# Final scaling of a decoder trunk: two of the eight blocks moved from VectorE to ScalarE and GpSimd

## The chip, the cores and the metric

The kernel runs on one core of a Trainium2 chip. The metric is the device time of one execution in microseconds (us): the median of 3 runs. The profile is one execution, recorded instruction by instruction.

## The reference

Two decoder layers run over 512 positions with a model width of 1024. Each layer is a half feed-forward block, a mixer and another half feed-forward block, all added to the residual stream `x`; at the very end stands one more RMS norm with its own weights. The change is in that last step:

```python
def rmsnorm(x, w, eps=NORM_EPS):
    xf = x.astype(F32)
    y = xf * lax.rsqrt(jnp.mean(xf * xf, axis=-1, keepdims=True) + eps)
    return (y * w.astype(F32)).astype(x.dtype)

def reference(x, ...):
    for l in range(DEPTH):
        ...
        x = x + 0.5 * swiglu(rmsnorm(x, ffn_norm[l, 1]), ...)
    return rmsnorm(x, final_norm)
```

## The kernel before

The residual stream lies transposed in SBUF as `X`, 128 partitions x 8 blocks (`KB`) x 512 positions, float32: a block is 128 of the 1024 features, and a position is a column. The feature weights of the norm are then one value per partition (`PRM[:, w:w+1]`), and the reciprocal root of a position is the same for all partitions.

Each engine has one program written out by hand; they meet only at semaphores. Weights are loaded by SyncE (line 544), copied to a high part by ScalarE (`split_hi`, L1340) and to a low part by VectorE (`split_lo`, L1989), and multiplied by TensorE in three products (L614 to L616). The last feed-forward block delivers the eight blocks of `X` one after another. For each, VectorE adds the product to `X` (L2001), ScalarE squares it into `US` (L1350) and GpSimd adds the square to `ACC` (L1855); the square of the last block is not added there but summed straight from `US`.

After the last block comes a tail in which each step waits for the one before: TensorE sums the squares over the partitions (L1318 for `ACC`, L1322 for the last block), VectorE adds the two (L2669), ScalarE takes the root (L1842), VectorE the reciprocal (L2671), and TensorE spreads the 512 results over all partitions into a PSUM bank called `ROWS`, which is `GATE[0]` (L1326, semaphore `rows_ready`). Then VectorE makes each output block `HF[:, m, :]` in one instruction (L2675), and SyncE stores the blocks in order, each when it is ready (L593), and waits for the last one to land.

`GS` is a buffer in SBUF that the feed-forward blocks use for the gate and which is free at this point. `HF` takes the place of `H`, which is free too.

ScalarE loads the table of the root ahead of time, before the last block (L1499).

Of the kernel before, what the change touches and what calls it, by code (L numbers as in the profile page):

```python
# [6 lines left out]
ALU = mybir.AluOpType  # L7
ACT = mybir.ActivationFunctionType
# [7 lines left out]
KB = D_MODEL // P  # L16
# [131 lines left out]
def hybrid_trunk_kernel(nc, x, params, const, w_gate, w_up, w_down, ab_in, ab_out, lru_a, lru_x,  # L148
# [18 lines left out]
    n_norms = len(plan) + 1  # L167
    norm_cols = []
# [8 lines left out]
    with ExitStack() as ctx:  # L177
# [4 lines left out]
        def at(name, offset, shape, dtype=F32):  # L182

            words = int(np.prod(shape[1:]))
            assert offset + words <= arena_words, name
            return nc.alloc_sbuf_tensor_at(name, list(shape), dtype, offset=arena_at + 4 * offset)
# [14 lines left out]
        X = at("X", X_AT, [P, KB, SEQ])  # L201
        H = at("H", H_AT, [P, 2, KB, SEQ], F32R)
        H_PARTS = (H[:, 0], H[:, 1])
        HF = at("HF", H_AT, [P, KB, SEQ])
# [3 lines left out]
        GS = at("GS", TMP_AT, [P, 2, SEQ])  # L208
# [4 lines left out]
        PRM = at("PRM", PARAM_AT, [P, NPARAM])  # L213
# [18 lines left out]
        def sem(name):  # L232
            return ctx.enter_context(nc.semaphore(name))
# [23 lines left out]
        out_ready, stored = sem("out_ready"), sem("stored")  # L257
# [4 lines left out]
        def fits(value):  # L262

            return not isinstance(value, int) or value > 0
# [49 lines left out]
        SDEC = at("SDEC", SPARE_AT + SEQ + 96, [P, 4, CHUNK])  # L314
        KEEP = at("KEEP", SPARE_AT + SEQ + 96 + 4 * CHUNK, [P, 14])
        LAST_ROOT, LAST_RSTD, LAST_SUM, ROWS = SMALL[:, 0, :], SMALL[:, 1, :], SMALL[:, 3, :], GATE[0]
        first_sums, first_copied, sums_added, rows_ready = (sem(k) for k in ("first_sums", "first_copied", "sums_added", "rows_ready"))
        LRU_SCALE = SMALL[:, 15, :]
        LRU_NSCALE = SMALL[:, 14, :]
# [15 lines left out]
        def ab_mix(t):  # L335

            return (12, 13, *range(4, 8), *range(4), *range(8, 12))[t - 4]
# [201 lines left out]
        @block.sync  # L539
        def _(sp):  # L540
            def load(u, slot, src, cols):
                if fits(u - RING + 1):
                    sp.wait_ge(lo_ready, u - RING + 1)
                sp.dma_start(RAW[:, slot, 0:cols], src).then_inc(w_landed[slot], 16)

            sp.dma_start(PRM[:, :], params).then_inc(x_landed[0], 16)
            load(0, 0, *units[0])
            for i in range(KB // 2):
                sp.dma_start(X[:, 2 * i:2 * i + 2, :], x[:, 2 * i:2 * i + 2, :]).then_inc(x_landed[i], 16)
                if i == 0:  # L550
                    load(1, 1, *units[1])
            load(2, 2, *units[2])
            sp.dma_start(CST[:, :], const).then_inc(landed, 16)
            for phase in plan:
                u0 = base[phase]
                if phase.startswith("ffn"):
                    n = int(phase[3])
                    for j in range(0 if u0 else 3, 4):
                        load(u0 + j, (u0 + j) % RING, *units[u0 + j])
                    with sp.Fori(1, FB // 2) as i:  # L560
                        for j in range(4):
                            src = (w_gate, w_up)[j % 2][n, 2 * i + j // 2]
                            load(u0 + 4 * i + j, (u0 + j) % RING, src, KB * P)
                    u1 = u0 + 2 * FB
                    with sp.Fori(0, KB // 2) as i:
                        for j in range(4):
                            src = w_down[n, 2 * i + j // 2, :, (j % 2) * UNIT:(j % 2 + 1) * UNIT]
                            load(u1 + 4 * i + j, (u1 + j) % RING, src, UNIT)
                else:
                    count = AB_BLOCKS if phase == "ab" else C_BLOCKS  # L570
                    for j in range(count + KB):
                        if phase == "ab" and j == RING:

                            sp.wait_ge(unit_done, u0)
                            for half in range(2):
                                rows = slice(half * CHUNK, (half + 1) * CHUNK)
                                sp.wait_ge(lw_zero, 1)
                                for k, w in enumerate((lru_a, lru_x)):
                                    sp.dma_start(LW[rows, k, :, rows], w[half]).then_inc(small_weights, 16)
                            sp.dma_start(WA2[:, :], rwkv_wa).then_inc(small_weights, 16)  # L580
                            sp.dma_start(G2[:, :], rwkv_g).then_inc(small_weights, 16)
                        if phase == "c" and j == RING:
                            sp.wait_ge(unit_done, u0)
                            sp.dma_start(CT[:, :, :], c_tail).then_inc(c_tail_landed.sem, 16)

                        if phase == "ab" and j == count:
                            for s in range(2):

                                sp.wait_ge(xx_mm[s], 10)
                        load(u0 + j, (u0 + j) % RING, *units[u0 + j])  # L590
            for m in range(KB):
                sp.wait_ge(out_ready, m + 1)
                sp.dma_start(out[m], HF[:, m, :]).then_inc(stored, 16)  # L593
            sp.wait_ge(stored, 16 * KB)

# [735 lines left out]
        def _(act):  # L1331
# [10 lines left out]
            def square(n, i, j):  # L1342

                if j == 0 and fits(KB // 2 * n + i):
                    act.wait_ge(acc_ready[0], KB // 2 * n + i)
                if j == 1 and fits(odd_sums(n) + i):
                    act.wait_ge(acc_ready[1], odd_sums(n) + i)
                    if n:
                        act.wait_ge(sum_ready, n)
                act.activation(US[:, j, :], X[:, 2 * i + j, :], ACT.Square).then_inc(sq_ready[j], 1)  # L1350

            def residual(n, i, j):

                act.wait_ge(x_ready[j], KB // 2 * n + i + 1)
                square(n, i, j)
                if n < n_norms - 1:
                    act.wait_ge(hw_ready[j], KB // 2 * n + i + 1)
                    act.activation(H[:, 0, 2 * i + j, :], GS[:, j, :], ACT.Copy).then_inc(hhi_ready[j], 1)
# [68 lines left out]
            for i in range(KB // 2):  # L1427
                act.wait_ge(x_landed[i], 32 if i == 0 else 16)
                for j in range(2):
                    w = norm_cols[0] + 2 * i + j  # L1430
                    act.activation(H[:, 0, 2 * i + j, :], X[:, 2 * i + j, :], ACT.Copy,
                                   scale=PRM[:, w:w + 1]).then_inc(hhi_ready[j], 1)
# [12 lines left out]
            for phase in plan:  # L1445
# [55 lines left out]
                if phase == "ab":  # L1501
# [24 lines left out]
                    for t in range(1, AB_BLOCKS):  # L1526
# [7 lines left out]
                        if 4 <= t < 18:  # L1534
                            act.wait_ge(z_read, t + 1)
                            if t == 14:
                                act.wait_ge(norm_sum_mm, 4)
                            act.activation(ab_place(t), PAD[:, t % 2, 3:3 + SEQ], ACT.Copy,
                                           scale=KEEP[:, ab_mix(t):ab_mix(t) + 1]).then_inc(z_kept, 1)
# [289 lines left out]
                if phase in ("ab", "c"):  # L1829

                    c0 = base[phase] + (AB_BLOCKS if phase == "ab" else C_BLOCKS)
                    act.wait_ge(mixer_done[phase], 1)
                    for m in range(KB):
                        if m < 2:
                            split_hi(c0 + m + 4, 0, done=c0 + m + 1)
                        elif m in (4, 5):
                            split_hi(c0 + m + 2, 0)
                        elif m >= 6 and c0 + m + 2 < n_units:
                            split_hi(c0 + m + 2, 0)
                        residual(norm_of[phase] + 1, m // 2, m % 2)  # L1840
            act.wait_ge(sums_added, 1)
            act.activation(LAST_ROOT, LAST_SUM, ACT.Sqrt, bias=EPS, scale=1.0 / D_MODEL).then_inc(rms_ready, 1)  # L1842


        @block.gpsimd
        def _(pool):
# [10 lines left out]
            def clear(n):  # L1857
                if n:
                    pool.wait_ge(sum_ready, n)
                pool.memset(ACC[:, :], 0.0).then_inc(acc_clear, 1)  # L1860
                pool.wait_ge(acc_clear, n + 1)

            def squares(n):

                clear(n)
                for j in range(2):
                    residual(n, 0, j)
                with pool.Fori(1, KB // 2 - 1) as i:
                    for j in range(2):
                        residual(n, i, j)  # L1870
                residual(n, KB // 2 - 1, 0)
                if 0 < n < n_norms - 1:
                    pool.wait_ge(h_ready[1], KB // 2 * (n + 1))
                    residual(n, KB // 2 - 1, 1)
# [44 lines left out]
            for phase in plan:  # L1919
# [52 lines left out]
                if phase == "c":  # L1972
                    pool.wait_ge(*c_silu(C_BLOCKS))
                squares(norm_of[phase] + 1)


        @block.vector
        def _(vec):
# [90 lines left out]
            for i in range(KB // 2):  # L2069
                for j in range(2):  # L2070
                    w = norm_cols[0] + 2 * i + j
# [598 lines left out]
            vec.wait_ge(rms_ready, n + 1)  # L2670
            vec.reciprocal(LAST_RSTD, LAST_ROOT).then_inc(rstd_ready, 1)  # L2671
            vec.wait_ge(rows_ready, 1)
            for m in range(KB):
                w = norm_cols[n] + m
                vec.scalar_tensor_tensor(HF[:, m, :], X[:, m, :], PRM[:, w:w + 1], ROWS[:, :],  # L2675
                                         ALU.mult, ALU.mult).then_inc(out_ready, 1)


# [16 lines left out]
```

## Time and profile before

| | |
|---|---|
| median of 3 runs | 2102.22 us (2101.36 to 2102.86) |
| span of the profiled execution, first to last instruction | 2102.0 us |
| TensorE busy | 2062.4 us, 98% |
| VectorE, ScalarE, GpSimd busy | 54%, 37%, 8% |
| last TensorE product of the weights ends | about 2089.7 us |
| first output block begun, last output block done by VectorE | 2094.02 us, 99.38 us after 2000 |

The profile gives the span of its execution, and no time of its own beside it; the median of the runs is 0.22 us above the span. The last product of the weights ends some 12.3 us before the end of the span: that is the tail of the kernel, and the change is made there. A row of the timeline gives start, duration, engine, line and operation, out<-in, shape and, in brackets, how long the engine had been idle and who ended that.

### The profile page before, as it was taken

The page shows a single profiled execution, that of the slowest core. Times are in us where ns is not written, and L with a number is a line of the kernel's source. Part 1 is how long each engine was busy: PE and PEld are TensorE (multiplying, and loading weights), DVE is VectorE, ACT ScalarE, POOL GpSimd, SP SyncE. Part 2 cuts the span into 40 slices and gives each one's busy share as a digit, 9 for nine tenths or more (in the row PEclk, how much of TensorE's full clock was granted, in tenths as well). Part 3 has the DMA queues.
Part 4 walks back from the last instruction along what each step waited for, and adds up shares of the span by engine and source line. Part 5 has one row for each costly group of instructions (what it writes and reads, how often), then busy time and mean ns, then how long its engine had stood idle before and what let it go on. Part 6 is the DMA issues. An engine that isn't in the chain of part 4 may idle for free.

```text
span 2102.0 us, 33182 instructions
## 1 busy us (share of the span) xinstructions
PE 2062.4 (98%) x13322; PEld 1699.5 (81%) x13322; DVE 1131.0 (54%) x1463; ACT 780.5 (37%) x1182; POOL 160.7 (8%) x118
## 2 busy tenths in 40 slices
PE   8999999999799999999999999999999999999998
PEld 6888888777768888888888888877888888888886
DVE  6444444678767444444444443469777675444322
ACT  5233223483434223322323232246665453233221
POOL 0000011002302000011000001101111120000010
PEclk9999999999999999999999999999999999999999
DMA  5222322320022222322222232221111122222321
GB/s 183 100 93 97 113 96 81 106 78 14 11 74 91 100 99 91 115 97 89 91 94 95 100 109 98 86 80 62 51 51 42 58 86 99 100 90 100 111 97 52
DMA packets 48265, 182.65 MB, mean 87 GB/s; under 512 B 6320, under 2 KB 6576, under 8 KB 48048
## 3 DMA queue, kind: packets, MB, share of 16 engines
q1 hardware_dynamic: 48176, 181.39, 25.1%
q8 instruction: 65, 1.06, 0.2%
q14 instruction: 24, 0.20, 0.0%
HBM read 179.27 MB, written 2.10 MB: 86 GB/s over the span
## 4 chain that ended last, share of the span: by engine, by line
PE 69%; DVE 2%; ACT 1%; issue 0%; POOL 0%; DVEq 0%; ACTq 0%; POOLq 0%
PE banks L614 21%; PE banks L615 21%; PE banks L616 21%; PE banks L1225 1%; PE banks L1194 0%; PE banks L1176 0%; PE banks L1264 0%; PE banks L1047 0%; PE banks L1266 0%; PE banks L1245 0%; PE banks L1242 0%; PE banks L1150 0%; PE banks L1130 0%; PE banks L1006 0%; DVE WS L1989 0%
## 5 line engine op out<-in xcount | busy, mean ns | idle before, releaser
L614 PE MATMUL banks<-H,WS 128*128 128x512 f32 x1840 | 727.6, 395 | 8.4 <-DVE H L2073 8.0
L615 PE MATMUL banks<-H,WS 128*128 128x512 f32 x1840 | 717.0, 390 | 0.0
L616 PE MATMUL banks<-H,WS 128*128 128x512 f32 x1840 | 716.9, 390 | 0.0
L1340 ACT ACTIVATE WS<-RAW 128x1024 fp32r<-128x1024 f32 (+1 forms) x306 | 345.0, 1128 | 909.4 <-PE banks L616 905.5
L1989 DVE TENSOR_TENSOR WS<-RAW,WS 128x1024 fp32r<-128x1024 f32 (+1 forms) x306 | 400.9, 1310 | 193.6 <-ACT WS L1340 193.2
L614 PEld LDWEIGHTS banks<-H,WS 128*128 128x128 f32 x1840 | 345.7, 188 | 85.1 <-DVE WS L1989 9.2
L616 PEld LDWEIGHTS banks<-H,WS 128*128 128x128 f32 x1840 | 345.7, 188 | 72.5
L615 PEld LDWEIGHTS banks<-H,WS 128*128 128x128 f32 x1840 | 345.9, 188 | 70.2 <-issue 1.2
L614 PE MATMUL banks<-A,WS 128*128 128x512 f32 x704 | 273.9, 389 | 0.0
L616 PE MATMUL banks<-A,WS 128*128 128x512 f32 x704 | 273.9, 389 | 0.0
L615 PE MATMUL banks<-A,WS 128*128 128x512 f32 x704 | 273.9, 389 | 0.0
L2029 DVE TENSOR_TENSOR US<-banks,RSTD 128x512 f32<-128x512 f32 x88 | 60.8, 691 | 252.2 <-PE banks L616 252.2
L1855 POOL TENSOR_TENSOR ACC<-ACC,US 128x512 f32<-128x512 f32 x47 | 87.5, 1862 | 1402.5 <-issue 763.0
L2029 DVE TENSOR_TENSOR GS<-banks,RSTD 128x512 f32<-128x512 f32 x88 | 60.8, 691 | 179.9 <-PE banks L616 179.8
L614 PEld LDWEIGHTS banks<-A,WS 128*128 128x128 f32 x704 | 132.1, 188 | 27.5
L616 PEld LDWEIGHTS banks<-A,WS 128*128 128x128 f32 x704 | 132.1, 188 | 27.5
L615 PEld LDWEIGHTS banks<-A,WS 128*128 128x128 f32 x704 | 132.1, 188 | 27.3
L2001 DVE SCALAR_TENSOR_TENSOR X<-banks,X 128x512 f32 (+1 forms) x48 | 33.0, 688 | 159.2 <-PE banks L616 159.2
L1380 ACT ACTIVATE A<-US 128x512 f32 (+1 forms) x88 | 55.8, 634 | 46.9 <-DVE US L2036 46.6
L2036 DVE TENSOR_TENSOR US<-GS,US 128x512 f32<-128x512 f32 x88 | 60.9, 692 | 9.1
L2041 DVE TENSOR_TENSOR A<-US,A 128x512 f32 (+1 forms) x88 | 60.2, 685 | 2.8 <-ACT A L1380 2.8
L1375 ACT ACTIVATE GS<-GS 128x512 f32<-128x512 f32 x88 | 54.1, 615 | 10.7 <-DVE GS L2029 10.7
(406 smaller groups left out, 1657.6 us busy)
## 6 DMA issues: line engine op xcount, KB each, us to landing
RAW<-in_w_gate SPq DMA_DIRECT2D x88, 512.0 KB, 3.2
RAW<-in_w_up SPq DMA_DIRECT2D x88, 512.0 KB, 3.2
RAW<-in_w_down SPq DMA_DIRECT2D x64, 704.0 KB, 4.0
RAW<-in_c_in SPq DMA_DIRECT2D x32, 512.0 KB, 3.2
RAW<-in_ab_in SPq DMA_DIRECT2D x22, 512.0 KB, 3.2
RAW<-in_ab_out SPq DMA_DIRECT2D x8, 512.0 KB, 5.0
RAW<-in_c_out SPq DMA_DIRECT2D x8, 512.0 KB, 3.2
X<-in_x SPq DMA_DIRECT2D x4, 512.0 KB, 7.5
```

What stands on the lines that cost most here:

```text
L614: pe.matmul(bank[:, :], high[:, cols], upper, start=first and j == 0, stop=False)
L615: pe.matmul(bank[:, :], high[:, cols], lower, start=False, stop=False)
L616: mm = pe.matmul(bank[:, :], low[:, cols], upper, start=False, stop=last and j == len(rows) - 1)
L1340: act.activation(WS[:, 0, c % SPLIT, 0:cols] if dst is None else dst, RAW[:, c % RING, 0:cols], ACT.Copy).then_inc(hi_ready, 1)
L1375: act.activation(GS[:, j, :], GS[:, j, :], ACT.Silu).then_inc(silu_ready[j], 1)
L1380: act.activation(A[:, 0, 2 * i + j, :], US[:, j, :], ACT.Copy).then_inc(ahi_ready[j], 1)
L1855: pool.tensor_tensor(ACC[:, :], ACC[:, :], US[:, j, :], ALU.add).then_inc(acc_ready[j], 1)
L1989: vec.tensor_tensor(WS[:, 1, c % SPLIT, 0:cols], RAW[:, c % RING, 0:cols], WS[:, 0, c % SPLIT, 0:cols].bitcast(F32), ALU.subtract).then_in ...
L2001: vec.scalar_tensor_tensor(X[:, 2 * i + j, :], bank[:, :], factor, X[:, 2 * i + j, :], ALU.mult, ALU.add).then_inc(x_ready[j], 1)
L2029: vec.tensor_tensor((GS, US)[k][:, j, :], (GATE, UP)[k][j][:, :], RSTD[:, :], ALU.mult).then_inc((gs_ready, us_ready)[k][j], 1)
L2036: vec.tensor_tensor(US[:, j, :], GS[:, j, :], US[:, j, :], ALU.mult).then_inc(prod_ready[j], 1)
L2041: vec.tensor_tensor(A[:, 1, 2 * i + j, :], US[:, j, :], A[:, 0, 2 * i + j, :].bitcast(F32), ALU.subtract).then_inc(act_ready[j], 1)
```

## The change

Blocks 5 and 6 (`POOL_SCALED`) are taken from VectorE's loop. ScalarE multiplies them by the feature weights into `HF`, behind its last square and ahead of its root. When the spread rows are there, ScalarE copies them from PSUM to `GS[:, 0, :]`. GpSimd multiplies the two blocks by `GS` in place. VectorE makes the other six, and reads the rows from `GS` in place of the PSUM bank, so it waits for the copy. SyncE stores the blocks in the order 0, 1, 2, 5, 3, 4, 6, 7.

```diff
+        POOL_SCALED = (KB - 3, KB - 2)
+        DVE_SCALED = (0, 1, 2, 3, 4, KB - 1)
 ...
-            for m in range(KB):
-                sp.wait_ge(out_ready, m + 1)
+            for m in (0, 1, 2, POOL_SCALED[0], 3, 4, POOL_SCALED[1], KB - 1):
+                if m in POOL_SCALED:
+                    sp.wait_ge(pool_scaled, POOL_SCALED.index(m) + 1)
+                else:
+                    sp.wait_ge(out_ready, DVE_SCALED.index(m) + 1)
                 sp.dma_start(out[m], HF[:, m, :]).then_inc(stored, 16)
 ...
+            for m in POOL_SCALED:
+                act.activation(HF[:, m, :], X[:, m, :], ACT.Copy, scale=PRM[:, norm_cols[n_norms - 1] + m:norm_cols[n_norms - 1] + m + 1]).then_inc(half_scaled, 1)
             act.wait_ge(sums_added, 1)
             act.activation(LAST_ROOT, LAST_SUM, ACT.Sqrt, bias=EPS, scale=1.0 / D_MODEL).then_inc(rms_ready, 1)
+            act.wait_ge(rows_ready, 1)
+            act.activation(GS[:, 0, :], ROWS[:, :], ACT.Copy).then_inc(rows_copied, 1)
 ...
+            pool.wait_ge(half_scaled, 2)
+            pool.wait_ge(rows_copied, 1)
+            for m in POOL_SCALED:
+                pool.tensor_tensor(HF[:, m, :], HF[:, m, :], GS[:, 0, :], ALU.mult).then_inc(pool_scaled, 1)
 ...
             vec.wait_ge(rows_ready, 1)
-            for m in range(KB):
+            vec.wait_ge(rows_copied, 1)
+            for m in DVE_SCALED:
                 w = norm_cols[n] + m
-                vec.scalar_tensor_tensor(HF[:, m, :], X[:, m, :], PRM[:, w:w + 1], ROWS[:, :],
+                vec.scalar_tensor_tensor(HF[:, m, :], X[:, m, :], PRM[:, w:w + 1], GS[:, 0, :],
                                          ALU.mult, ALU.mult).then_inc(out_ready, 1)
```

## Rows read from the trace of the kernel before

**Rows 1.** The page: its first lines.

```profile
span 2102.0 us, 33182 instructions
...
PE 2062.4 (98%) x13322; PEld 1699.5 (81%) x13322; DVE 1131.0 (54%) x1463; ACT 780.5 (37%) x1182; POOL 160.7 (8%) x118
```

**Rows 2.** Timeline of the tail: start us, us, engine line op out<-in [idle before <-releaser].

```profile
2089.77 0.69 DVE L2001 SCALAR_TENSOR_TENSOR X<-banks,X 128x512 f32<-128x512 f32 x1 [11.86 <-PE banks L616]
2090.50 0.63 ACT L1350 ACTIVATE US<-X 128x512 f32<-128x512 f32 x1 [12.21 <-DVE X L2001]
...
2092.34 0.16 DVE L2669 TENSOR_TENSOR SMALL<-SMALL,banks 128x4 f32<-128x4 f32 x1 [1.62 <-PE banks L1322]
2092.53 0.20 ACT L1842 ACTIVATE SMALL<-SMALL 128x4 f32<-128x4 f32 x1 [1.41 <-DVE SMALL L2669]
2092.77 0.18 DVE L2671 RECIPROCAL SMALL<-SMALL 128x4 f32<-128x4 f32 x1 [0.27 <-ACT SMALL L1842]
...
2093.01 0.97 PE L1326 MATMUL banks<-CST,SMALL 128*128 128x128 f32 x4 [0.77 <-DVE SMALL L2671]
2094.02 5.36 DVE L2675 SCALAR_TENSOR_TENSOR HF<-X,PRM,banks 128x512 f32<-128x512 f32 x8 [1.07 <-PE banks L1326]
2094.79 4.94 SPq L593 DMA_DIRECT2D out_dram<-HF  x8
```

**Rows 3.** The tile HF: duration min/median/max ns, and issue to landing.

```profile
L2675 DVE SCALAR_TENSOR_TENSOR HF<-X,PRM,banks x8: 740/740/746, 2094.0 to 2098.6; 128x512 f32<-128x512 f32 x8
L593 SPq DMA_DIRECT2D out_dram<-HF x8: 332/332/353, 2094.8 to 2099.4; - x8
...
DMA to landing us min/median/max: 2.0/2.1/2.2
```

**Rows 4.** Waits of SyncE's DMA queue in the tail.

```profile
SPq L177 <- DMA out_dram<-HF: 1.9, 1, 1.9
```

**Rows 5.** Windows of the tail: the last three columns are granted clock, DMA share, GB/s.

```profile
2095.75:2101.00 5.25, 0.00 (x0) 0.00 (x0) 3.62 (x6) 0.00 (x0) 0.00 (x0) 0.50 1.01 381
```

**Rows 6.** Lines of ScalarE: one copy out of PSUM, duration min/median/max ns.

```profile
L1742 ACT ACTIVATE c_XX<-banks x16: 598/598/601, 1451.9 to 1659.2; 128x512 f32<-128x512 f32 x16
```

**Rows 7.** Timeline of ScalarE: four scaled by a column, and copies around a root.

```profile
445.29 2.55 ACT L1571 ACTIVATE KKSQ<-KF,PRM 128x512 f32<-128x512 f32 x4
...
665.62 1.28 ACT L1369 ACT_TABLE_LOAD   x1
667.68 0.60 ACT L1369 ACTIVATE RSTD<-banks 128x512 f32<-128x512 f32 x1 [0.78 <-PE banks L649]
669.10 1.06 ACT L1340 ACTIVATE WS<-RAW 128x1024 fp32r<-128x1024 f32 x1 [0.83 <-PE banks L616]
670.18 1.28 ACT L1375 ACT_TABLE_LOAD   x1
```

**Rows 8.** Timeline of VectorE and GpSimd: each with the other engine's SBUF reads absent.

```profile
498.88 2.73 DVE L2269 SCALAR_TENSOR_TENSOR T<-FACTORS,PRM,KF 128x512 f32<-128x512 f32 x4
...
519.79 4.96 POOL L1892 TENSOR_TENSOR GG<-XC,GG 128x512 f32<-128x512 f32 x4
```

**Rows 9.** Timeline near 2076 us: GpSimd begins while VectorE is at work.

```profile
2076.16 0.61 ACT L1350 ACTIVATE US<-X 128x512 f32<-128x512 f32 x1
2076.29 1.63 DVE L1989 TENSOR_TENSOR WS<-RAW,WS 128x1408 fp32r<-128x1408 f32 x1 [0.78 <-ACT WS L1340]
...
2076.85 2.20 POOL L1855 TENSOR_TENSOR ACC<-ACC,US 128x512 f32<-128x512 f32 x1 [12.81 <-ACT US L1350]
```

**Rows 10.** Timeline near 640 us: VectorE begins while GpSimd is at work.

```profile
639.63 1.28 POOL L1855 TENSOR_TENSOR ACC<-ACC,US 128x512 f32<-128x512 f32 x1 [3.11 <-ACT US L1350]
...
640.02 1.45 DVE L2015 TENSOR_TENSOR H<-GS,H 128x512 fp32r<-128x512 f32 x1 [0.70 <-ACT H L1358]
```

**Rows 11.** Timelines near 1436 and 1447 us: both engines with a queue.

```profile
1435.79 2.50 DVE L2452 SCALAR_TENSOR_TENSOR KQV<-PAD,PRM,KQV 128x512 f32<-128x512 f32 x2
...
1436.44 1.30 POOL L1951 TENSOR_TENSOR c_TM<-c_TTH,CST 128x512 f32<-128x512 f32 x1 [53.30 <-ACT c_TTH L1723]
1437.82 1.62 POOL L1953 TENSOR_TENSOR c_TM<-c_TM,CST 128x512 f32<-128x512 f32 x1
...
1446.87 0.75 DVE L2458 SCALAR_TENSOR_TENSOR KQV<-PAD,PRM,KQV 128x512 f32<-128x512 f32 x1
1447.54 1.54 DVE L2464 SCALAR_TENSOR_TENSOR KQV<-TANH,KQV 128x512 f32<-128x512 f32 x1
...
1447.16 2.83 POOL L1965 TENSOR_TENSOR c_KDT<-c_KDT,TL 128x512 f32<-128x512 f32 x2 [2.85 <-PE banks L1176]
```

More of the change, by code:

```diff
@@ L316, in hybrid_trunk_kernel @@
         LAST_ROOT, LAST_RSTD, LAST_SUM, ROWS = SMALL[:, 0, :], SMALL[:, 1, :], SMALL[:, 3, :], GATE[0]
+        POOL_SCALED = (KB - 3, KB - 2)
+        pool_scaled, half_scaled = sem("pool_scaled"), sem("half_scaled")
+        DVE_SCALED = (0, 1, 2, 3, 4, KB - 1)
+        rows_copied = sem("rows_copied")
         first_sums, first_copied, sums_added, rows_ready = (sem(k) for k in ("first_sums", "first_copied", "sums_added", "rows_ready"))
```

## The prediction, made before the changed kernel ran

> **What bounds the kernel now.** I read the page first. TensorE is busy for 98% of a span of 2102.0 us [rows 1]; the change touches no product of the weights, so only what follows the last one can move, and that is the tail. I then read the timeline of the tail [rows 2]. It is a strict chain: the add of block 7, its square, the sums, the root, the reciprocal, the spread rows at 2093.98 (2093.01 + 0.97), and from 2094.02 eight VectorE instructions until 2099.38 (2094.02 + 5.36). From there it seems that VectorE sets the end, with 8 blocks one behind the other. One starts every (5.36 - 0.74) / 7 = 0.660 us [rows 2, 3].
>
> The third view, the windows, says more. From 2095.75 to 2101.00 the DMA share is 1.01 at 381 GB/s [rows 5]: the 16 DMA engines are full from shortly after the first store to shortly before the last lands. A block is 128 x 512 x 4 = 262,144 bytes, and at 381 GB/s that takes 0.688 us. VectorE delivers a block every 0.660 us and the DMA engines take one every 0.688, so the stores set the end, and VectorE merely keeps ahead of them. The landings agree: 2.0 us from issue for the quickest and 2.2 for the slowest, which is 7 x 0.028 = 0.2 of queue built up [rows 3]. So I use this rule for the end: the last landing is the issue of the first store of an unbroken series + 2.0 + 0.688 for each further store in it. Before: 2094.79 + 2.0 + 7 x 0.688 = 2101.61. The wait of 1.9 us for the last store from about 2099.7 (the end of the queue's row, 2094.79 + 4.94) gives the same 2101.6 [rows 2, 4]. Some 0.4 us follow to the end of the span.
>
> What counts for the change is therefore when the first blocks are stored and whether the stores then come without a gap. How soon VectorE has finished counts little.
>
> **ScalarE's two early multiplications.** Four of the same shape with a scale per partition take 2.55 us, 0.71 each and 0.61 from start to start [rows 7]. The last square ends at 2091.13, the sums are there at 2092.50 (2092.34 + 0.16) [rows 2]. The two run from about 2091.04 to 2091.04 + 0.61 + 0.71 = 2092.36. They are hidden behind TensorE's sums, with 0.17 us to spare before the root at 2092.53; if that cover were gone, at most 1.3 us would be added. I take nothing. They are ready long before GpSimd needs them. Between root and copy ScalarE has nothing else.
>
> **The copy of the rows.** This step is new on the path, as both VectorE and GpSimd wait for it. A PSUM copy of this shape takes 0.60 us [rows 6], and a hand-over to the next engine 0.04 (2093.98 to 2094.02) [rows 2]. VectorE starts at 2094.02 + 0.60 + 0.04 = 2094.66 in place of 2094.02: 0.64 later. Nothing hides it, and nothing is queued for VectorE meanwhile. The first store goes out 0.77 after VectorE's start [rows 2], at 2095.43. SyncE waits behind it for everything else.
>
> **VectorE's six.** With all operands in SBUF, four of this instruction take 2.73 us, or (2.73 - 0.75) / 3 = 0.66 from start to start [rows 8]. Reading the rows from SBUF in place of PSUM gives nothing by itself. Two fewer save 1.32 us of VectorE.
>
> **GpSimd's two, and what they do to VectorE.** Alone, a product of this shape takes 4.96 / 4 = 1.24 us [rows 8]. But when VectorE reads two tensors from SBUF at the same time, the trace shows them taking turns:
> - GpSimd begins at 2076.85 while VectorE's subtraction of two SBUF tensors runs to 2077.92 (2076.29 + 1.63). It ends at 2079.05, and so takes 2.20 in place of 1.28, and 1.13 of it after VectorE is done [rows 9].
> - VectorE begins at 640.02 while GpSimd works until 640.91, and ends at 641.47: 1.45 in place of 0.69, with 0.56 after GpSimd is done [rows 10].
> - With queues on both sides they alternate. The second of two VectorE instructions, of the very form of this change, is held up while a GpSimd product runs; it ends at 1438.29, 0.55 after that product's 1437.74, and the next GpSimd product ends at 1439.44, 1.15 later. Near 1447 a VectorE instruction takes 1.54 between two back-to-back GpSimd ones [rows 11].
>
> Before the change each of the eight had only one tensor input in SBUF (`X`; the rows were in PSUM). After it, all six have two, `X` and `GS`, and so the eight blocks go through one gate. VectorE is first, as GpSimd starts 0.08 after ScalarE's end [rows 9] and VectorE 0.04. Turn by turn: block 0 ends at 2095.40; block 5 (GpSimd) at 2095.40 + 1.13 = 2096.53; block 1 at + 0.55 = 2097.08; block 6 at + 1.13 = 2098.21; block 2 at + 0.55 = 2098.76; blocks 3, 4 and 7 at 0.66 each: 2099.42, 2100.08, 2100.74. VectorE ends 1.4 us later than before, with two blocks fewer.
>
> The Trainium skill, SBUF — State Buffer, section Who interferes with whom, says that a VectorE instruction with two SBUF inputs and a GpSimd instruction that reads SBUF exclude each other for the whole instruction. It speaks against this change, and the trace agrees on the exclusion. By its whole instruction each turn of GpSimd would cost 1.24 in place of the 1.13 seen behind a VectorE end, and the time below would be some 0.2 us more.
>
> **The stores.** They are issued 0.03 after a block is done (2094.79 for an end at 2094.76), and one issue takes 0.33 us [rows 2, 3]. Block 0 goes at 2095.43, block 1 at 2097.11, block 2 at 2098.79, then 5 at 2099.13, 3 at 2099.47, 4 at 2100.11, 6 at 2100.44 and 7 at 2100.77. The order puts block 5 behind block 2, though it is ready at 2096.53. The DMA engines stand idle between the first three, and from 2098.79 six stores run without a break: 2098.79 + 2.0 + 5 x 0.688 = 2104.23. The last store by itself would land at 2102.8, so the series decides. Against 2101.61 that is **+2.6 us**. The predicted span is 2104.6, and against the median of the runs 2102.22 + 2.6 = **2104.8 us**, 0.12% more.
>
> Other orders of the turns hardly change it. If GpSimd's two go back to back behind block 0, block 1 ends at 2095.40 + 1.13 + 1.24 + 0.55 = 2098.32; seven stores from 2098.35 land at 2104.48, +2.9. If GpSimd is kept waiting until VectorE's six are done (2098.7), block 5 is ready at 2099.83 and holds up SyncE; five stores from 2099.86 land at 2104.6, +3.0.
>
> **Rivals.**
> - *No turns taken: the six and the two run side by side.* Block 7 would be done at 2094.66 + 5 x 0.66 + 0.74 = 2098.70, 0.7 sooner than now, and GpSimd's at 2097.2. That is how the change would bring a gain. But the stores begin 0.64 later and are 8 x 0.688 as ever: 2095.43 + 2.0 + 7 x 0.688 = 2102.25, so even then +0.6, or 2102.9. For it: in the early part of a GpSimd instruction some overlap is seen (1.13 for 1.24). Against it: [rows 9 to 11]. Chance 0.12.
> - *VectorE's end decides, and the DMA engines could take more than 381 GB/s.* With no turns taken the end would be 0.7 sooner, 2101.5. Against it: a share of 1.01 [rows 5]. Chance 0.03.
> - *Slower by more than the measurement can miss: ScalarE changes its tables.* If `Copy` needed a table other than that of the root, a load of 1.28 would come ahead of the two multiplications and one ahead of the root. The two would end at 2091.13 + 1.28 + 1.32 = 2093.73, the root would begin at 2095.01 in place of 2092.53, and the load for the copy is hidden in the wait for the rows. That is +2.5 on top of +2.6: 2107.3. It decides from 1.6 us on, as 0.2% is 4.2 us. Against it: after the root at 667.68 a copy runs at 669.10 with no load between [rows 7]. For it: only that the copy with a scale per partition is not seen right after a root. Chance 0.03.
> - *Turns as above:* chance 0.82.
>
> **How the numbers follow.** A change of 0.2%, 4.2 us, is about what a measurement of this kernel can tell from none. The turns give +2.6 to +3.0, and the medians of a few runs vary by some 0.5 (the runs shown spread from 2101.36 to 2102.86). Their own range is 2104.0 to 2105.9. The range to hold 8 in 10 reaches down toward the case without turns: 2103.0 to 2106.0. Faster by over 0.2% (under 2098.0) needs something that no row shows: 0.01. Slower by over 0.2% (over 2106.4) has the tables and an unlucky median: 0.05. Within 0.2%: 0.94.
>
> **What the profile would show.** The first `HF` instruction of VectorE at 0.64 later than the rows; two of the six at 1.3 to 1.8 us in place of 0.74; GpSimd's two at over 1.3 us, with one of VectorE's ends between them; a gap in the DMA share between the first stores and a share near 1 from about 2099 on; a first store some 0.64 later and the last landing near 2104.2. No table load behind 2078. The prediction is wrong if VectorE's six all take 0.74 (then +0.6), or if the series of stores is faster than 0.688 each.

## The result, and the profile after

The changed kernel takes 2104.76 us (median of 21 runs, 2104.29 to 2106.22), the kernel before, run beside it, 2102.03 (21 runs, 2101.16 to 2103.33). That is 2.7 us more; the ratio is 1.0014, with a 95% interval of 1.0008 to 1.0020. The prediction was 2104.8, a rise of 2.6, and "within 0.2%" the likeliest of the three.

The timeline of the tail after the change answers to [rows 2]:

```profile
2090.11 1.05 PE L1329 MATMUL banks<-CST,US 128*128 128x1 f32 x8 [0.66 <-ACT US L1357]
...
2091.27 0.16 DVE L2684 TENSOR_TENSOR SMALL<-SMALL,banks 128x4 f32<-128x4 f32 x1 [1.62 <-PE banks L1329]
2091.46 0.21 ACT L1851 ACTIVATE SMALL<-SMALL 128x4 f32<-128x4 f32 x1 [0.18 <-DVE SMALL L2684]
...
2091.93 0.65 PE L1333 MATMUL banks<-CST,SMALL 128*128 128x128 f32 x4 [0.77 <-DVE SMALL L2686]
2092.62 0.60 ACT L1853 ACTIVATE GS<-banks 128x512 f32<-128x512 f32 x1 [0.95 <-PE banks L1333]
2093.34 6.15 DVE L2691 SCALAR_TENSOR_TENSOR HF<-X,PRM,GS 128x512 f32<-128x512 f32 x6 [1.46 <-ACT GS L1853]
2093.36 2.93 POOL L1989 TENSOR_TENSOR HF<-HF,GS 128x512 f32<-128x512 f32 x2 [15.38 <-ACT GS L1853]
2095.20 5.45 SPq L600 DMA_DIRECT2D out_dram<-HF  x8
```

Six VectorE instructions take 6.15 us where eight took 5.36, and the first store is issued 2.62 behind the rows (2095.20 against 2092.58) where it was 0.81 (2094.79 against 2093.98). The tile `HF` shows which instructions are long, and answers to [rows 3]; the columns are duration min/median/max in ns, then the first and last start:

```profile
L600 SPq DMA_DIRECT2D out_dram<-HF x8: 333/451/644, 2095.2 to 2100.0; - x8
L2691 DVE SCALAR_TENSOR_TENSOR HF<-X,PRM,GS x6: 741/743/1833, 2093.3 to 2098.7; 128x512 f32<-128x512 f32 x6
L1849 ACT ACTIVATE HF<-X,PRM x2: 706/706/707, 2090.0 to 2090.6; 128x512 f32<-128x512 f32 x2
L1989 POOL TENSOR_TENSOR HF<-HF,GS x2: 1262/1486/1709, 2093.4 to 2094.6; 128x512 f32<-128x512 f32 x2
```

The median of the six is 0.743 us, so most are as they were; the same view cut to the stretch from 2093 to 2096 shows that the first two are the long ones:

```profile
L2691 DVE SCALAR_TENSOR_TENSOR HF<-X,PRM,GS x2: 1745/1789/1833, 2093.3 to 2095.1; 128x512 f32<-128x512 f32 x2
```

With the two of GpSimd that gives the turns: GpSimd from 2093.36 to 2094.62; VectorE, which had started at 2093.34, ends at 2095.17, 0.55 later; GpSimd's second ends at 2096.29 after 1.71 in all, 1.12 of it behind 2095.17; VectorE's second at 2096.84, 0.55 later again. Block 5 is done first, then block 0, 6 and 1.

The DMA view from 2093 to 2105, in 40 slices of 0.3 us (tenths of the 16 DMA engines), and two windows, one from inside its hole to just behind it and one over the long series that follows, which answer to [rows 5] (the last three columns are granted clock, DMA share and GB/s):

```profile
DMA  0000000000795002999999999999999700000000
```

```profile
2097.40:2098.10 0.70, 0.00 (x0) 0.00 (x0) 0.70 (x3) 0.00 (x0) 0.00 (x0) 0.50 0.55 208
2098.30:2102.40 4.10, 0.00 (x0) 0.00 (x0) 1.19 (x2) 0.00 (x0) 0.00 (x0) 0.50 1.03 383
```

The first store runs alone, then the engines stand idle for 0.6 to 0.9 us, and then the other seven stores run as one series at 383 GB/s, against 381 before. The last lands at about 2103.05: SyncE waits for it for 2.4 us from the end of its queue's row (2095.20 + 5.45).

```profile
SPq L177 <- DMA out_dram<-HF: 2.4, 1, 2.4
```

**How small differences are read here.** The runs of one kernel spread over 2 us and more, and most of that lies ahead of the tail: in the traces of this study the rows are there anywhere from 2091.7 us (kernel 1 below) to 2093.98 (the kernel before). So besides the medians I use the length of the tail, from the moment the rows are there (the end of the transposes that spread them) to the end of the span. With the times of the traces to the nanosecond, of which the views print fewer digits, it is 2102.024 - 2093.978 = 8.05 us before and 2103.402 - 2092.585 = 10.82 after. That difference, 2.8, is near the 2.7 of the medians.

### The profile page after: what moved, and what is told of

It reads as the page before. It is cut to its first block, busy times and chain, and to the rows that moved or that the text cites. A ratio compares the mean times of both kernels' runs of the same rounds, so it can differ in the third digit from the quotient of the medians.

```text
span 2103.4 us, 33187 instructions
## 1 busy us (share of the span) xinstructions
PE 2061.3 (98%) x13322; PEld 1699.2 (81%) x13322; DVE 1132.2 (54%) x1461; ACT 782.6 (37%) x1185; POOL 163.6 (8%) x120
## 4 chain that ended last, share of the span: by engine, by line
PE 69%; DVE 2%; ACT 1%; issue 0%; POOL 0%; DVEq 0%; ACTq 0%; POOLq 0%
PE banks L621 21%; PE banks L622 21%; PE banks L623 21%; PE banks L1232 1%; PE banks L1201 0%; PE banks L1183 0%; PE banks L1271 0%; PE banks L1054 0%; PE banks L1273 0%; PE banks L1252 0%; PE banks L1249 0%; PE banks L1157 0%; PE banks L1137 0%; PE banks L1013 0%; DVE WS L2004 0%
```

## The experiments

Eight kernels were run, each 11 times, with the kernel before on the same chip (medians of 2102.2 to 2102.4). The tail lengths come from one trace each, to the nanosecond as above, and nothing here measures how much the tail of one kernel varies from run to run. The ratios are not the quotients of two medians: for kernel 3 those would give 1.0005. By the ratios, only the change and kernels 6 and 8 are clear of no difference; the steps from one kernel to the next rest mainly on the traces.

| kernel | median | ratio to before, 95% interval | tail | against 8.05 |
|---|---|---|---|---|
| the change | 2104.76 | 1.0014 (1.0008 to 1.0020) | 10.82 | +2.8 |
| 1: rows from PSUM, with GpSimd | 2102.76 | 1.0003 (0.9994 to 1.0012) | 8.76 | +0.7 |
| 2: and no wait for the copy | 2102.07 | 0.9999 (0.9990 to 1.0008) | 8.09 | 0.0 |
| 3: the copy alone | 2103.35 | 1.0002 (0.9993 to 1.0011) | 8.75 | +0.7 |
| 4: other order of stores | 2103.61 | 1.0008 (0.9999 to 1.0017) | 9.56 | +1.5 |
| 5: kernel 2 with six stores | 2100.75 | 0.9991 (0.9982 to 1.0000) | 6.74 | -1.3 |
| 6: GpSimd one block later | 2104.89 | 1.0011 (1.0002 to 1.0020) | 9.99 | +1.9 |
| 7: before with six stores | 2102.18 | 0.9999 (0.9990 to 1.0008) | 7.89 | -0.2 |
| 8: VectorE 0.1 us earlier | 2104.88 | 1.0012 (1.0003 to 1.0021) | 10.62 | +2.6 |

**1. The rows from PSUM, with GpSimd beside VectorE.**

```diff
-                vec.scalar_tensor_tensor(HF[:, m, :], X[:, m, :], PRM[:, w:w + 1], GS[:, 0, :],
+                vec.scalar_tensor_tensor(HF[:, m, :], X[:, m, :], PRM[:, w:w + 1], ROWS[:, :],
```

> The changed kernel, but VectorE's six read the rows from the PSUM bank again, while they still wait for ScalarE's copy. Each then has one tensor in SBUF. Theory (turns at SBUF): no turns are taken, all six take 0.74 us and GpSimd's two 1.24 to 1.28; VectorE still starts 0.7 late, the eight stores run without a gap, and the last one lands 0.7 later than in the kernel before: +0.7 us, about 2102.7. Rival 1 (GpSimd disturbs VectorE whatever VectorE reads): as the changed kernel, +2.7. Rival 2 (VectorE's end decides, not the stores): block 7 is done 0.6 sooner than before, so -0.6.

The tile `HF` of this kernel:

```profile
L2691 DVE SCALAR_TENSOR_TENSOR HF<-X,PRM,banks x6: 742/744/747, 2092.5 to 2095.8; 128x512 f32<-128x512 f32 x6
...
L1989 POOL TENSOR_TENSOR HF<-HF,GS x2: 1262/1262/1263, 2092.5 to 2093.7; 128x512 f32<-128x512 f32 x2
```

Both engines work at the same time, on the same blocks as in the changed kernel, and nothing is held up: no instruction of VectorE takes over 0.747, none of GpSimd over 1.263. The one thing that differs is where VectorE's second tensor lies. (In the changed kernel that is also the very buffer that GpSimd reads, `GS`; but [rows 9] show a turn with no tensor in common, `RAW` and `WS` against `ACC` and `US`, so sharing a buffer is not needed for it.) The tail is 2.1 us shorter than the changed kernel's, the median 2.0, and the slowest run here (2103.93) is under the fastest of the change (2104.29). Rival 1 falls. VectorE is done 4.8 us behind the rows (2092.48 + 4.04 = 2096.52 against 2091.72), 0.6 sooner than before, and yet the tail is 0.7 longer: rival 2 falls too.

**2. And no wait for the copy.** TensorE spreads the rows once more into `GATE[1]`, since ScalarE and VectorE would otherwise read one bank with nothing to order them.

```diff
+            for j in range(TT):
+                mm = pe.transpose(GATE[1][:, j * P:(j + 1) * P], LAST_RSTD[:, j:j + 1].to_broadcast([P, P]), con("ident"))
+            mm.then_inc(rows_ready, 1)
...
-            act.wait_ge(rows_ready, 1)
-            act.activation(GS[:, 0, :], ROWS[:, :], ACT.Copy).then_inc(rows_copied, 1)
+            act.wait_ge(rows_ready, 2)
+            act.activation(GS[:, 0, :], GATE[1][:, :], ACT.Copy).then_inc(rows_copied, 1)
...
-            vec.wait_ge(rows_copied, 1)
```

> As the first, and VectorE does not wait for the copy either: TensorE spreads the rows a second time into another bank, and ScalarE copies from that one. VectorE starts at its old time with six blocks in place of eight, GpSimd makes two beside it. Theory (the stores set the end): VectorE is done some 1.3 us sooner than in the kernel before, the first store goes out at the old time, and the last lands at the old time: within 0.1 us of the kernel before in the tail, ratio 1.000. Rival (VectorE's end decides): -1.3 us in the tail.

The timeline of its tail:

```profile
2092.10 4.04 DVE L2693 SCALAR_TENSOR_TENSOR HF<-X,PRM,banks 128x512 f32<-128x512 f32 x6 [1.21 <-PE banks L1333]
2092.88 4.52 SPq L600 DMA_DIRECT2D out_dram<-HF  x8
...
2093.70 2.50 POOL L1992 TENSOR_TENSOR HF<-HF,GS 128x512 f32<-128x512 f32 x2 [16.70 <-ACT GS L1856]
```

VectorE is done 4.04 us after it begins, in place of 5.36, and GpSimd at 2096.20, 4.1 after. All eight blocks are there 1.2 us sooner than before, counted from the rows, and the tail is 8.09 against 8.05. This is what the change would have had at its best: nothing.

**3. The copy alone**, with VectorE making all eight blocks from it:

```diff
+            act.wait_ge(rows_ready, 1)
+            act.activation(GS[:, 0, :], ROWS[:, :], ACT.Copy).then_inc(rows_copied, 1)
...
             vec.wait_ge(rows_ready, 1)
+            vec.wait_ge(rows_copied, 1)
...
-                vec.scalar_tensor_tensor(HF[:, m, :], X[:, m, :], PRM[:, w:w + 1], ROWS[:, :],
+                vec.scalar_tensor_tensor(HF[:, m, :], X[:, m, :], PRM[:, w:w + 1], GS[:, 0, :],
```

> The kernel before with the copy alone: ScalarE copies the rows to SBUF, VectorE waits for it and makes all eight blocks from the copy, with two tensors in SBUF each; GpSimd does nothing. Theory: two SBUF inputs cost nothing without GpSimd, so all eight take 0.74 us, and the copy costs 0.7 us: +0.7. Rival (the form with two SBUF inputs is slow by itself): the eight take longer than 0.74 each and the cost comes near +2.7.

```profile
L2679 DVE SCALAR_TENSOR_TENSOR HF<-X,PRM,GS x8: 746/748/751, 2092.9 to 2097.5; 128x512 f32<-128x512 f32 x8
```

Two tensors in SBUF cost nothing as long as GpSimd reads none: 0.75 for all eight. The tail is 8.75, and the copy's price 0.7. With kernel 1 this closes the square: neither VectorE's two SBUF inputs nor GpSimd's work is dear alone, only both together.

**4. The stores in the order in which the blocks are done.**

```diff
-            for m in (0, 1, 2, POOL_SCALED[0], 3, 4, POOL_SCALED[1], KB - 1):
+            for m in (POOL_SCALED[0], 0, POOL_SCALED[1], 1, 2, 3, 4, KB - 1):
```

> The changed kernel with the stores issued in the order in which the blocks were done in its trace: 5, 0, 6, 1, 2, 3, 4, 7. The turns stay. Theory (an unbroken series of stores sets the end): the first store goes out 0.55 us sooner, the one for block 6 fills the gap between blocks 0 and 1, and the last lands some 1.2 us sooner than in the changed kernel: +1.5 us against the kernel before. Rival (the end hangs on VectorE's last block alone): no gain over the changed kernel, +2.7.

The timeline and the tile `HF`:

```profile
2092.90 6.15 DVE L2691 SCALAR_TENSOR_TENSOR HF<-X,PRM,GS 128x512 f32<-128x512 f32 x6 [1.92 <-ACT GS L1853]
...
2094.22 5.20 SPq L600 DMA_DIRECT2D out_dram<-HF  x8
```

```profile
L2691 DVE SCALAR_TENSOR_TENSOR HF<-X,PRM,GS x6: 739/740/1834, 2092.9 to 2098.3; 128x512 f32<-128x512 f32 x6
```

The turns are the same to 0.01 us, with the same 6.15 for the six, and the tail is 1.3 us shorter. So 1.3 of the 2.8 was not in VectorE's delay itself but in stores that waited behind it: block 5 is done 2.04 behind the rows and was stored in fourth place.

**5 and 7. Six stores in place of eight**, from kernel 2 and from the kernel before. Both leave out the stores of blocks 5 and 6, so two eighths of the output are not written.

```diff
-            for m in (0, 1, 2, POOL_SCALED[0], 3, 4, POOL_SCALED[1], KB - 1):
+            for m in DVE_SCALED:
...
-            sp.wait_ge(stored, 16 * KB)
+            sp.wait_ge(pool_scaled, 2)
+            sp.wait_ge(stored, 16 * len(DVE_SCALED))
```

> The second kernel (no wait for the copy, rows spread twice) with the stores of blocks 5 and 6 left out, so that two eighths of the output are not written; all eight blocks are still computed. Theory (each store costs 0.69 us of the end, and VectorE's end nothing): the last of six stores lands 2 x 0.69 = 1.37 us sooner than in the kernel before and than in the second kernel, counted from the moment the rows are first there. Rival (the end of the second kernel hangs on something else, such as GpSimd's blocks or the number of issues): the gain is clearly smaller.

```diff
             for m in range(KB):
                 sp.wait_ge(out_ready, m + 1)
-                sp.dma_start(out[m], HF[:, m, :]).then_inc(stored, 16)
-            sp.wait_ge(stored, 16 * KB)
+                if m not in (KB - 3, KB - 2):
+                    sp.dma_start(out[m], HF[:, m, :]).then_inc(stored, 16)
+            sp.wait_ge(stored, 16 * (KB - 2))
```

> The kernel before with the stores of blocks 5 and 6 left out, so that two eighths of the output are not written; VectorE still makes all eight. Theory: the stores set the end of the kernel before by only 7 x 0.028 = 0.2 us over VectorE, so that without two stores VectorE takes over at once, and the last landing is only 0.2 us sooner. Rival (stores alone count, VectorE is far from the bound): 1.37 us sooner.

Their timelines, kernel 5 and then kernel 7:

```profile
2092.32 4.04 DVE L2691 SCALAR_TENSOR_TENSOR HF<-X,PRM,banks 128x512 f32<-128x512 f32 x6 [0.74 <-PE banks L1331]
...
2093.09 3.62 SPq L597 DMA_DIRECT2D out_dram<-HF  x6
```

```profile
2092.41 5.36 DVE L2676 SCALAR_TENSOR_TENSOR HF<-X,PRM,banks 128x512 f32<-128x512 f32 x8 [1.21 <-PE banks L1327]
2093.18 5.00 SPq L594 DMA_DIRECT2D out_dram<-HF  x6
```

With six blocks from VectorE, two stores fewer take 1.3 us off the tail (6.74 against 8.09 and 8.05), or 0.65 to 0.68 each. With eight blocks from VectorE the same saves only 0.16 (7.89), since its last block is done no sooner. In the kernel before both limits lie that close together: 8 x 0.688 us of stores, and VectorE 0.2 us under it. Take away either one alone and nothing is gained.

**6. GpSimd one block later.**

```diff
             pool.wait_ge(rows_copied, 1)
+            pool.wait_ge(out_ready, 1)
```

> The changed kernel, but GpSimd also waits until VectorE has finished block 0. The turns are as many, two, but they fall behind blocks 1 and 2 in place of ahead of 0 and 1. Theory (what counts is when the first stores go out and whether they leave a gap): blocks 0 and 1 are stored from 1.5 us behind the rows on, the gaps are filled in part, and the last store lands about 0.75 us sooner than in the changed kernel, +2.0 us against the kernel before. Rival (the sum of the work at the gate is all that counts): no gain, +2.7.

```profile
2093.74 6.07 DVE L2692 SCALAR_TENSOR_TENSOR HF<-X,PRM,GS 128x512 f32<-128x512 f32 x6 [1.81 <-ACT GS L1853]
2094.52 5.98 SPq L600 DMA_DIRECT2D out_dram<-HF  x8
2094.67 3.28 POOL L1990 TENSOR_TENSOR HF<-HF,GS 128x512 f32<-128x512 f32 x2 [16.62 <-DVE HF L2692]
```

The first store goes out 1.53 behind the rows in place of 2.62, and the tail is 9.99, 0.8 shorter than the changed kernel's, as expected. The median does not show it (2104.89, runs between 2103.48 and 2105.31, against 2104.76 for the change). By its one trace the theory holds; by the time of the runs this one is inconclusive.

**8. VectorE 0.1 us earlier.**

```diff
-            vec.wait_ge(rows_ready, 1)
             vec.wait_ge(rows_copied, 1)
```

> The changed kernel without VectorE's wait for the rows in PSUM, which the wait for the copy covers anyway. In the changed kernel's trace VectorE starts 0.12 us behind the copy and 0.03 ahead of GpSimd, and yet GpSimd has the first turn. Theory a (the second wait costs 0.08 us, and with 0.1 us of lead VectorE has the first turn, as the prediction had it): VectorE starts 0.04 behind the copy, block 0 takes 0.74 and goes out at 1.45 in place of 2.61 behind the rows, blocks 1 and 2 take 1.7 each, and the last store lands some 0.2 us sooner than in the changed kernel. Theory b (GpSimd wins the first turn even so): block 0 takes 1.8 to 1.9 again and nothing else moves.

```profile
2093.43 0.60 ACT L1853 ACTIVATE GS<-banks 128x512 f32<-128x512 f32 x1 [1.17 <-PE banks L1333]
2094.06 6.07 DVE L2690 SCALAR_TENSOR_TENSOR HF<-X,PRM,GS 128x512 f32<-128x512 f32 x6 [1.59 <-ACT GS L1853]
2094.17 3.43 POOL L1989 TENSOR_TENSOR HF<-HF,GS 128x512 f32<-128x512 f32 x2 [15.59 <-ACT GS L1853]
2094.84 6.41 SPq L600 DMA_DIRECT2D out_dram<-HF  x8
```

The tile `HF` in the stretch from 2094.0 to 2094.7, where block 0 alone is at work, and for the whole tail:

```profile
L2690 DVE SCALAR_TENSOR_TENSOR HF<-X,PRM,GS x1: 750/750/750, 2094.1 to 2094.1; 128x512 f32<-128x512 f32 x1
```

```profile
L1989 POOL TENSOR_TENSOR HF<-HF,GS x2: 1704/1733/1762, 2094.2 to 2095.9; 128x512 f32<-128x512 f32 x2
```

VectorE now starts 0.03 behind the copy and 0.11 ahead of GpSimd, and has the first turn: block 0 takes 0.75, and both of GpSimd's are held up. The tail is 10.62, 0.2 shorter, which the median (2104.88 against 2104.76) can't show. By the trace theory a held, and this kernel is the one that the prediction had worked out turn by turn.

No version that writes the whole output beats the kernel before: the best, kernel 2, is level with it.

## Why the prediction was right, point by point

**What bounds the tail.** Right. Kernel 2 finishes all blocks 1.2 us sooner and ends level; kernels 5 and 7 measure the price of a store (0.65 to 0.68) and the distance to VectorE's limit (0.16, where I had 0.2).

**ScalarE's two early multiplications at nothing.** Right. They take 0.706 each and end at 2091.28, 0.14 ahead of the sums at 2091.43 and 0.18 ahead of the root at 2091.46. I had 0.17. No table load appears; the rival with tables is out.

**The copy at 0.64.** The copy took its 0.60. The hand-over to VectorE was 0.12 and not 0.04, so the step cost 0.7. Kernel 3 gives 0.7 for it alone. The missed part is that VectorE now waits twice in a row, for the rows and then for the copy, which I had costed at nothing; with the wait for the copy alone (kernel 8) the hand-over is 0.03. GpSimd, which also has two waits, started 0.14 behind the copy and not 0.08.

**The turns.** Right in kind and in price: VectorE ended 0.55 behind a GpSimd end twice, and GpSimd 1.12 behind a VectorE end once (its first was not held up); in kernel 8 both of GpSimd's were, each for 1.12. VectorE's six span 6.15 us, and the steps of the prediction, from 2094.66 to 2100.74, make 6.08. Kernel 1 shows that the turns come from the second SBUF tensor beside a reading GpSimd, and kernel 3 that it takes GpSimd. The SBUF rule of the Trainium skill (SBUF — State Buffer, Who interferes with whom) holds for this instruction too. The exclusion is there, but a turn costs less than the whole instruction: GpSimd's took 1.26 where nothing held it up and 1.12 behind a VectorE end, and my 1.13 was the better of the two prices that the prediction named.

**Who is first.** Wrong. I had VectorE first, as its hand-over is shorter. GpSimd was, though it started 0.02 later. That moved block 0 from 1.42 to 2.59 behind the rows. The prediction's list of other orders does not have this one, but its terms give nearly the same sum for it: block 5 would be done at 2095.94, block 0 at 2096.49, block 6 at 2097.62 and block 1 at 2098.17, and seven stores from 2098.20 would land at 2104.33, +2.7 in place of +2.6. Kernel 8, with the order that was predicted, has +2.6 against the change's +2.8. So the number survived a wrong order because both orders cost about the same, which the prediction had not worked out for this one: that is luck in part.

**The stores.** The rule (2.0 us from the first issue of an unbroken series, and 0.688 for each further store) was right. The last series of the changed kernel has seven stores, from block 1 on: 2096.87 + 2.0 + 6 x 0.688 = 2103.00, and SyncE's wait for the last landing ends at 2103.05. In kernel 8 it has six, from block 2 at 2098.18, as the prediction had it, and the rule gives 2103.62, which is also the last landing in its trace. I took 0.33 us for every issue. A store issued right behind another took more: the row of L600 above has a median of 0.451 and a longest of 0.644. It cost nothing, since the DMA engines still had work queued.

**The sum.** +2.6 predicted, +2.8 in the tail, +2.7 in the medians. What the parts are worth can be told from the kernels: 0.7 for the copy (kernel 3), and 2.1 for the turns (the change against kernel 1), of which 1.3 come from the order of the stores (kernel 4).

**The base.** The prediction put the median 0.2 us above the span. In every run here whose span is listed, the time is 1.7 to 1.9 us above it, so the profiled execution of the kernel before must have been one of some 2103.8, slower than the median. This cost nothing, as only the difference of two spans was used; whoever had added up parts of the kernel would have been off by 1.6.

**The rivals.** No turns: kernel 1 shows that rival's world, and its +0.6 comes out at +0.7 in the tail. VectorE's end decides: falls with kernels 1 and 2.

## What to carry to other kernels

When a chain of equal blocks is computed and stored, compare the pace of both before you speed up one: here a block took 0.660 us to make and 0.688 to store, so a helper for the making could not gain (kernel 2), and where the stores ran as one series a delay of the first was paid in full (kernels 1 and 3). Before you give GpSimd part of an elementwise job, look at where VectorE's second tensor lies: out of PSUM the two ran side by side at full pace, out of SBUF they took turns, and each GpSimd turn cost 1.1 to 1.3 us. And once blocks come from two engines, a store queue that works in a fixed order should take them in the order in which the trace shows them done; that alone was worth 1.3 of the 2.8 us.

## What the hardware did that was not expected

- A start 0.02 us ahead did not give VectorE the first turn; a start 0.11 ahead did. In the change and in kernel 4, with a lead of 0.02 both times, GpSimd was first, and VectorE's first instruction took 1.83 us. Where between the two the turn changes hands, and why, was not tested.
- Two waits in a row, the first of them fulfilled long before the second, delayed VectorE's next instruction by about 0.08 us against one wait (0.12 against 0.03 from ScalarE's end to VectorE's start).
- The four transposes that spread the rows took 0.65 us after the change and 0.97 in [rows 2]. The windows show a granted clock of 1.00 for the stretch of the one and 0.76 for that of the other, so part of it fell to the lower of the two levels in the kernel before. In both traces the engine had been at full work until its last product of the weights, 3.3 us before the spread began, and in between had only summed the squares, for some 1.8 us of the 3.3; why the clock had fallen by then in the one and not in the other is not shown. First the kernel before, then after:

```profile
2092.30:2094.00 1.70, 0.97 (x4) 0.57 (x4) 0.34 (x2) 0.20 (x1) 0.00 (x0) 0.76 0.00 0
```

```profile
2091.20:2092.60 1.40, 0.65 (x4) 0.41 (x4) 0.34 (x2) 0.29 (x2) 0.00 (x0) 1.00 0.00 0
```

The same step took 0.65 to 1.12 in the other traces, with no pattern between the kernels. It ends before the rows are there, so it is not in the tails compared above, and it can account for up to 0.5 us of the spread of the runs.
